# Small decay and rate products in pairs behind the first eight gate tiles of a two-block network

## The chip, the cores and the metric

The kernel runs on one core of one Trainium2 chip. The metric is the device time of one launch in microseconds; lower is better. The core has a matrix engine (TensorE, PE in the profile, its weight loads PEld), a vector engine (VectorE, DVE), an activation engine (ScalarE, ACT), GpSimd (POOL) and SyncE (SP), which issues most DMAs. Each engine works through its own instruction stream in order; engines wait for one another through semaphores.

## The reference

Two blocks run one after the other on a sequence of 1024 tokens of 1024 features, in float32. The second block is where the change lies. Cut to what matters, it starts like this:

```python
h = rmsnorm_2(x, g_mix)
z = h @ w_in                      # 1024 x 5384
zf = z[..., :1544]                # attention ("fox"): q, k, v and 8 forget columns
zr = z[..., 1544:3336]            # recurrence ("rwkv"), 1792 columns
zg = z[..., 3336:]                # two gates of 1024 columns
y_fox = fox_attention(q, k, v, log_sigmoid(zf[..., 1536:] + b_f))
zr = zr + mu_shift * (token_shift(zr) - zr)
dw, da = zr[..., 1536:1600], zr[..., 1600:1664]
w_log = -softplus(-(w0 + tanh(dw) @ w_decay_up)) - 0.5   # decay, 64 -> 512
a = sigmoid(a0 + da @ w_aaa_up)                          # rate, 64 -> 512
y_rwkv = rwkv7_scan(...) ...
merged = sigmoid(zg[..., :1024]) * (y_fox @ w_o_fox) + sigmoid(zg[..., 1024:]) * (y_rwkv @ w_o_rwkv)
x = x + merged @ w_out            # then a feed-forward part and an embedding part
```

The two products with inner size 64 (`dw`, `da`) are the small decay and rate products of the title. All else of the block stays as it is.

## The kernel before, in words

Large products are made in three passes of 512 columns (high weights by high data, low weights by high data, high weights by low data), so a tile of 128 features by 512 tokens with 8 slices of the inner dimension takes 24 matmuls (lines 469 to 471, helper `pe_fm`). Weights come in pieces of 1 MB: SP loads one (`sp_load`, line 407), ACT copies its high part (`ac_cut`, line 420), DVE subtracts to get the low part (`ve_cut`, line 430), and PE may use it. A piece feeds four tiles.

Stage `a4` makes all of `z` in this order: attention columns (`first`), recurrence columns (`shift`, 28 tiles), the small products (`lora`: 16 tiles, four feature groups by two token halves by decay and rate), and the gates (`gates`, 32 tiles, numbered 0 to 31 here). For each small tile PE makes one product with 64 rows (line 2922), ACT takes it out of its PSUM bank with a Sigmoid (line 3033), DVE scales the decay ones (line 2976), and ACT issues a DMA to DRAM (line 3040). Results of `a4` are kept in eight staging slots, taken in turn by the number `no[key]`.

PSUM has 8 banks. A product takes the next bank of a ring (`Banks.take`): `RING` is banks 0 to 5, the gate tiles have a ring of their own (0, 1, 2, 3), the attention has `FB` = (4, 5, 6). Each ring has one place counter for the whole program, kept under the ring's tuple, so two users of the same tuple share a counter. Before it writes, PE waits until the bank's former result was taken out (`bk.room`).

While the gate tiles run, the attention is begun beside them. It is written as one generator for each engine (`pe_fox`, `ve_fox`, `ac_fox`, `po_fox`, `sp_fox`), whose steps count the same on all engines. Each gate tile takes three steps: on PE behind the slices 2, 5 and 7 of the tile, on DVE and ACT ahead of the tile's evacuation (line 2983) and its DMA (line 3048). The first steps are: 1 load and bias the forget columns (ACT line 3332, DVE 3292); 2 their log-sigmoid on ACT (3335 to 3339: Abs, Exp, Ln); 3 the cumulative sum on DVE (3296, 3298). Then, for each of four pairs of heads: rests; the norms of q and k (steps 6 to 13 of the first pair: ACT Square 3348, PE 3272, ACT Ln 3355 and Exp 3360, DVE 3311); then for each of eight query blocks the scores (PE 3152, DVE 3196 and 3201), the minimum (DVE 3208), the Exp (ACT 3228), the transposes (PE 3164) and the weighted sum (PE 3176). In all PE has 228 steps for four pairs, and a tail.

What is left of the attention at the end of `a4` runs in `b2` beside the recurrence. There each step of the other streams is followed by one slot of the attention, slowed so that step n of what is left comes in slot 2.5 n (rounded down):

```python
def slow(stream):
    for n, _ in enumerate(stream):
        yield
        yield
        if n % 2:
            yield
```

The loop of `b2` has 352 slots; the last 13 stand behind the steps of the recurrence's last scan (`ve_scan`, `ac_scan`, `pe_scan` of unit 7). Behind the attention comes its tail (`pe_tail`, `ve_tail`, `ac_tail`, `sp_tail`): rests, and then the first four output tiles of the next stage (`o_tiles[:4]`, PE lines 719 to 721, banks 4 to 7) from four parts, each with a high part (ACT 3445) and a low part (DVE 3435). What does not fit into the loop's slots runs behind it. Then all engines meet, and stage `a5` makes the other output tiles: its first four (`tiles[4:8]`) wait for room in the next four banks of `RING` and then for low parts (DVE 4102); DVE takes the four kept tiles out of banks 4 to 7 (line 4111) behind those low parts.

Of the kernel before, what the change touches and what calls it, by code (L numbers as in the profile page):

```python
# [10 lines left out]
ALU = mybir.AluOpType  # L11
ACT = mybir.ActivationFunctionType
# [231 lines left out]
def program(nc, D, out, S):  # L244
# [3 lines left out]
    with ExitStack() as ctx:  # L248
# [70 lines left out]
        def PC(name, k=0, p0=0, p1=128):  # L319
            return PB[p0:p1, pat[name] + k:pat[name] + k + 1]  # L320
# [16 lines left out]
        bk = Banks(PS, [sem(f"bank_filled{b}") for b in range(8)], [sem(f"bank_emptied{b}") for b in range(8)])  # L337
        RING, SUM0, SUM1 = (0, 1, 2, 3, 4, 5), (6,), (7,)
# [5 lines left out]
        s_o = [dma_sig(f"stage_out{i}") for i in range(8)]  # L344
# [324 lines left out]
        def span(hf):  # L669
            return slice(0, T) if hf is None else slice(512 * hf, 512 * hf + 512)  # L670
# [2184 lines left out]
        def a4(pe_fox, ve_fox, ac_fox, po_fox, sp_fox, load_first):  # L2855
# [6 lines left out]
            WU = AF[:, 10 * T + 6:10 * T + 518]  # L2862
            first = fm("fox_qk", "w_in_2", 0, 1024) + tm("fox_v", "w_in_2", 1024, 512, 8) + fm("fox_f", "w_in_2", 1536, 128)
            shift, gates = fm("shift", "w_in_2", 1544, 1792), fm("gates", "w_in_2", 3336, 2048)
            lora = [(j, hf, g) for j in range(4) for hf in range(2) for g in range(2)]
            no = {t.key: i for i, t in enumerate(first)}
            no.update({("lora",) + u: len(first) + i for i, u in enumerate(lora)})
            no.update({t.key: len(first) + 16 + i for i, t in enumerate(gates)})

            def stage(key):  # L2870
                return AF[:, 512 * (no[key] % 8):512 * (no[key] % 8 + 1)]

            def room(key):
                return s_o[no[key] % 8].at(no[key] // 8 - 1)
# [1 line left out]
            def stored(key):  # L2876
                return s_o[no[key] % 8].at(no[key] // 8)

            def three(stream):
                for _ in range(3):  # L2880
                    next(stream)

            def mix_sums(e):
# [21 lines left out]
            def pe_a4(e):  # L2905
                for n, t in enumerate(first):
                    if t.seg == "fox_v" and t.f + t.a == 0:
                        root_columns(e)
                    (pe_tm if t.seg == "fox_v" else pe_fm)(e, t, hp, parts_ready(2, None) if n == 0 else None)
                    if n == 1:  # L2910
                        mix_sums(e)
                    if n == 4:
                        out_sums(e)
                for t in shift:
                    pe_fm(e, t, hp)
                e.wait_ge(*lora_in.at(1))
                e.wait_ge(*sh_act.at(0))
                for j, hf, g in lora:
                    key = ("lora", j, hf, g)
                    ps, s_ = bk.take(key, RING), slice(64 * g, 64 * g + 64)  # L2920
                    e.wait_ge(*bk.room(key))
                    e.matmul(ps, WU[s_, j * 128:(j + 1) * 128], DD[s_, hf * 512:(hf + 1) * 512], start=True,
                             stop=True).then_inc(*bk.fill(key))
                for t in gates:
                    pe_fm(e, t, hp, None, (0, 1, 2, 3), pe_fox, (2, 5, 7))

            def ve_a4(e):
                ve_cut(e, first[0].j + 2)
# [25 lines left out]
                for t in shift:  # L2954
# [14 lines left out]
                    e.tensor_tensor(d, raw[:, 0:T], raw[:, 1:T + 1], ALU.subtract).then_inc(*vo.up())  # L2969
                    e.wait_ge(*vo.last())  # L2970
                    e.scalar_tensor_tensor(d, d, PC("mu_shift_2", t.f), raw[:, 1:T + 1], ALU.mult, ALU.add).then_inc(*sh_dif.up())
                for u in lora:
                    if u[2] == 0:
                        b = stage(("lora",) + u)
                        e.wait_ge(*bk.emptied(("lora",) + u))
                        e.tensor_scalar(b, b, -math.exp(-0.5), None, ALU.mult).then_inc(*lora_neg.up())
                for t in gates:
                    if t.first:
                        ve_cut(e, t.j + 2)
                    three(ve_fox)  # L2980
                    e.wait_ge(*bk.filled(t.key))
                    e.wait_ge(*room(t.key))
                    e.tensor_tensor(stage(t.key), bk[t.key], RR[:, span(t.hf)], ALU.mult).then_inc(*bk.empty(t.key))

            def ac_a4(e):
                ac_cut(e, first[0].j + 2)
# [10 lines left out]
                for n_, t in enumerate(first):  # L2997
# [5 lines left out]
                    n = t.m if t.seg == "fox_v" else 512  # L3003
# [9 lines left out]
                for t in shift:  # L3013
# [10 lines left out]
                        e.activation(d, d, ACT.Sigmoid).then_inc(*sh_act.up())  # L3024
                        e.wait_ge(*sh_act.at(1))
                    e.dma_start(S["zr"][t.f * 128:(t.f + 1) * 128, :], d).then_inc(*dif_out[0 if t.f == 13 else t.f % 2].up())
                scaled = 0
                for u in lora:
                    j, hf, g = u
                    key = ("lora",) + u  # L3030
                    e.wait_ge(*bk.filled(key))
                    e.wait_ge(*room(key))
                    e.activation(stage(key), bk[key], ACT.Sigmoid, bias=PC(("w0_2", "a0_2")[g], j)).then_inc(*bk.empty(key))
                    if g == 0:
                        e.wait_ge(*lora_neg.at(scaled))
                        scaled += 1
                    else:
                        e.wait_ge(*bk.emptied(key))
                    row = 512 * g + j * 128
                    e.dma_start(S["rw_d"][row:row + 128, hf * 512:(hf + 1) * 512], stage(key)).then_inc(*s_o[no[key] % 8].up())  # L3040
                for t in first[-2:]:
                    e.wait_ge(*stored(t.key))
                for t in gates:
                    if t.first:
                        ac_cut(e, t.j + 2)
                    three(ac_fox)
                    e.wait_ge(*bk.emptied(t.key))
                    e.dma_start(S["gates"][t.f * 128:(t.f + 1) * 128, t.hf * 512:(t.hf + 1) * 512],
                                stage(t.key)).then_inc(*s_o[no[t.key] % 8].up())

            def po_a4(e):
                e.wait_ge(*z_lo.at(piece(2, 7)))
                e.memset(AF[:, 4 * T:4 * T + 3078], 0.0).then_inc(*sh_pad.up())
                for t in gates:
                    three(po_fox)

            def sp_a4(e):
                e.dma_start(WU[0:64, :], D["w_decay_up_2"]).then_inc(*lora_in.up())
                e.dma_start(WU[64:128, :], D["w_aaa_up_2"]).then_inc(*lora_in.up())
                sp_load(e, shift[-1].j + 3)  # L3060
                e.wait_ge(*x_spilled.at(0))
                e.wait_ge(*bk.filled(shift[-1].key))
                for t in first[-8:]:
                    e.wait_ge(*stored(t.key))
                for n, t in enumerate(gates):
                    if t.first:
                        sp_load(e, t.j + 3)
                    three(sp_fox)
# [1361 lines left out]
```

## Time and profile before

| what | us |
|---|---|
| median of 3 runs | 4201.96 (4199.37 to 4202.57) |
| profiled execution, its own time | 4214.02 |
| its span | 4212.7 |
| PE busy | 3892.7 (92%) |
| DVE busy | 2257.0 (54%) |
| ACT busy | 1196.0 (28%) |
| POOL busy | 446.9 (11%) |

The profile shows one execution; its own time is longer than the median of the runs, so it is used for durations and differences, not for the total. In timeline rows the columns are: start in us from the span's start, duration in us, engine and line, operation, what it writes and reads, shapes, count, and in brackets the idle time before it and what ended that. "ACTq" and "SPq" are DMA issues of those engines. Shares of busy time are means over stages with different limits.

### The profile page before, as it was taken

Reading aid. Unit: us, or ns where it says so; the run is one execution under the profiler, and the core shown is the slowest. Engines: PE = TensorE matmul, PEld = TensorE weight load, DVE = VectorE, ACT = ScalarE, POOL = GpSimd, SP = SyncE. Lnnn points to the kernel's source line nnn. Section 1 sums busy time; section 2 is a strip of 40 time slices with the busy share of each in tenths; the row PEclk is TensorE's granted clock in tenths of the full one; section 3 lists DMA queues with packets and bytes.
Section 4 is the critical chain, followed back from the end, with each engine's and each line's share of the span. In section 5 each row is a group of like instructions: output and inputs, shape, how many; then the busy total and the mean of one; then the engine's idle time right before and its main releaser. Section 6 shows DMA issues by size and latency. Waiting matters only on the chain. (4 is left out here: it accounts for less than half of the span.)

```text
span 4212.7 us, 75887 instructions
## 1 busy us (share of the span) xinstructions
PE 3892.7 (92%) x33370; PEld 3190.3 (76%) x33370; DVE 2257.0 (54%) x3662; ACT 1196.0 (28%) x1700; POOL 446.9 (11%) x440
## 2 busy tenths in 40 slices
PE   6999969988999999999999898788888999999999
PEld 5888847777867788888798576566677788888877
DVE  4643335554434666766634233564544476676673
ACT  4221234433323433121400323333323321111132
POOL 0001103321000432000000001222212000000000
PEclk8999979997999999999999899886879999999999
DMA  5211120113121334322322322111004211111111
GB/s 181 82 61 57 57 93 7 33 33 134 40 80 70 104 114 168 130 86 82 118 88 90 131 84 68 56 36 45 23 30 163 89 41 50 50 44 47 50 46 65
DMA packets 228061, 318.71 MB, mean 76 GB/s; under 512 B 17149, under 2 KB 172541, under 8 KB 227605
## 3 DMA queue, kind: packets, MB, share of 16 engines
q1 hardware_dynamic: 199088, 251.13, 18.1%
q10 hardware_dynamic: 28644, 62.72, 3.9%
q8 instruction: 265, 4.34, 0.4%
q14 instruction: 64, 0.52, 0.0%
HBM read 235.46 MB, written 78.35 MB: 74 GB/s over the span
## 5 line engine op out<-in xcount | busy, mean ns | idle before, releaser
L469 PE MATMUL ps<-sb_a_h,sb_whi 128*128 128x512 f32 (+1 forms) x2336 | 932.7, 399 | 6.1 <-DVE sb_wlo L430 5.7
L471 PE MATMUL ps<-sb_a_h,sb_whi 128*128 128x512 f32 (+1 forms) x2336 | 915.5, 392 | 0.0
L470 PE MATMUL ps<-sb_a_h,sb_wlo 128*128 128x512 f32 (+1 forms) x2336 | 915.2, 392 | 0.0
L469 PEld LDWEIGHTS ps<-sb_a_h,sb_whi 128*128 128x128 f32 (+1 forms) x2336 | 441.8, 189 | 116.5 <-issue 16.3
L470 PEld LDWEIGHTS ps<-sb_a_h,sb_wlo 128*128 128x128 f32 (+1 forms) x2336 | 442.0, 189 | 95.2 <-issue 5.1
L471 PEld LDWEIGHTS ps<-sb_a_h,sb_whi 128*128 128x128 f32 (+1 forms) x2336 | 441.1, 189 | 95.2
L420 ACT ACTIVATE sb_whi<-sb_wraw 128x2048 fp32r<-128x2048 f32 (+3 forms) x132 | 233.7, 1771 | 810.2 <-PE ps L471 493.9
L675 DVE TENSOR_TENSOR sb_x<-sb_x,ps 128x512 f32<-128x512 f32 x480 | 314.8, 684 | 211.5 <-PE ps L471 196.5
L430 DVE TENSOR_TENSOR sb_wlo<-sb_wraw,sb_whi 128x2048 fp32r<-128x2048 f32 (+3 forms) x132 | 281.9, 2136 | 223.7 <-ACT sb_whi L420 203.2
L469 PE MATMUL ps<-sb_a_g,sb_whi 128*128 128x512 f32 x896 | 349.8, 390 | 11.5 <-DVE sb_x L675 10.5
L470 PE MATMUL ps<-sb_a_g,sb_wlo 128*128 128x512 f32 x896 | 348.7, 389 | 0.0
L471 PE MATMUL ps<-sb_a_g,sb_whi 128*128 128x512 f32 x896 | 348.6, 389 | 0.0
L469 PEld LDWEIGHTS ps<-sb_a_g,sb_whi 128*128 128x128 f32 x896 | 168.2, 188 | 50.6 <-DVE sb_x L675 14.7
L471 PEld LDWEIGHTS ps<-sb_a_g,sb_whi 128*128 128x128 f32 x896 | 168.2, 188 | 35.0
L470 PEld LDWEIGHTS ps<-sb_a_g,sb_wlo 128*128 128x128 f32 x896 | 168.2, 188 | 34.8
L4226 DVE TENSOR_TENSOR sb_a_f<-ps,sb_root 128x512 f32<-128x512 f32 x88 | 60.9, 692 | 101.8 <-PE ps L471 96.1
L3245 POOL TENSOR_TENSOR sb_b<-sb_x,sb_consts 128x128 f32<-128x128 f32 x64 | 30.0, 483 | 611.2 <-DMA sb_x<-fox_c 398.9
L4276 ACT ACTIVATE sb_a_g<-sb_a_f 128x512 fp32r<-128x512 f32 x44 | 27.8, 633 | 226.0 <-DVE sb_a_f L4246 226.0
L526 PE MATMUL ps<-sb_a_h,sb_whi_blocks 128*128 128x512 f32 x224 | 87.9, 392 | 4.0 <-DVE sb_wlo_blocks L552 4.0
L528 PE MATMUL ps<-sb_a_h,sb_whi_blocks 128*128 128x512 f32 x224 | 87.9, 392 | 0.0
L527 PE MATMUL ps<-sb_a_h,sb_wlo_blocks 128*128 128x512 f32 x224 | 87.7, 391 | 0.0
L719 PE MATMUL ps<-sb_a_h,sb_whi 128*128 128x512 f32 x128 | 56.4, 441 | 25.2 <-DVE sb_wlo L430 8.7
(589 smaller groups left out, 6692.0 us busy)
## 6 DMA issues: line engine op xcount, KB each, us to landing
sb_wraw<-w_in SPq DMA_DIRECT2D x33, 1024.0 KB, 5.3
sb_wraw<-w_ff SPq DMA_DIRECT2D x32, 1024.0 KB, 5.4
sb_wraw<-w_up SPq DMA_DIRECT2D x22, 1024.0 KB, 5.1
sb_wraw<-w_down SPq DMA_DIRECT2D x11, 1024.0 KB, 4.9
sb_wraw<-w_xkv SPq DMA_DIRECT2D x8, 1024.0 KB, 5.5
sb_wraw<-w_out SPq DMA_DIRECT2D x8, 1024.0 KB, 5.3
sb_b<-rw_d SPq DMA_DIRECT2D x16, 512.0 KB, 6.4
sb_b<-y SPq DMA_DIRECT2D x16, 512.0 KB, 5.8
```

The source lines that it names most:

```text
L420: e.activation(WH[j % 2][:, 0:m], WR[j % 2][:, 0:m], ACT.Copy).then_inc(s_whi, 1)
L430: e.tensor_tensor(WL[j % 2][:, 0:m], WR[j % 2][:, 0:m], WH[j % 2][:, 0:m].bitcast(F32), ALU.subtract).then_inc(s_wlo, 1)
L469: e.matmul(o, wh[:, k, c], xh[:, sl], start=(k == 0), stop=False)
L470: e.matmul(o, wl[:, k, c], xh[:, sl], start=False, stop=False)
L471: m = e.matmul(o, wh[:, k, c], xl[:, sl], start=False, stop=(k == t.nk - 1))
L526: e.matmul(o, wh[:, k, :], xhi, start=(opens and k == 0), stop=False, skip_group_check=True)
L527: e.matmul(o, wl[:, k, :], xhi, start=False, stop=False, skip_group_check=True)
L528: m = e.matmul(o, wh[:, k, :], xlo, start=False, stop=(k == 3), skip_group_check=True)
L675: e.tensor_tensor(o, o, bk[t.key], ALU.add).then_inc(*bk.empty(t.key))
L719: e.matmul(ps[n], wh[:, k, c], xh[:, sl], start=(i == 0), stop=False)
L3245: e.tensor_tensor(nms[g], R(NCB[g] + qb * 128, 128), C("causal"), ALU.subtract).then_inc(*fx_nm[g].up())
L4226: e.tensor_tensor(raw[:, 2:514], bk[t.key], RR[:, span(t.hf)], ALU.mult).then_inc(*bk.empty(t.key))
```

## The change

The 16 small tiles no longer stand between `shift` and `gates`. Gate tile 0 follows the shift tiles at once; behind each of the gate tiles 0 to 7 stands one pair (decay and rate of one feature group and token half), on every engine behind that tile's own work. The pairs use the ring (4, 5, 6), the attention's, in place of `RING`. On ACT both Sigmoids of a pair come first, then its two DMAs. Beside gate tile 0 only one step of the attention is taken (on PE behind slice 7); the other tiles take three as before, so the steps 2, 3, ... come two steps later in the order of gate tiles. The first load of the recurrence's inputs on SP moves from gate tile 8 to gate tile 12. The staging slots are numbered anew.

In `ve_a4` the scaling of a pair's decay tile moves behind the evacuation of gate tile n in the same way as the pair on ACT below, and `po_a4` and `sp_a4` take `fox_steps` in place of `three`. The diff's core, from the tables, `pe_a4`, `ac_a4` and `sp_a4`:

```diff
-            lora = [(j, hf, g) for j in range(4) for hf in range(2) for g in range(2)]
+            lora, LORA = [(j, hf, g) for j in range(4) for hf in range(2) for g in range(2)], (4, 5, 6)
             no = {t.key: i for i, t in enumerate(first)}
-            no.update({("lora",) + u: len(first) + i for i, u in enumerate(lora)})
-            no.update({t.key: len(first) + 16 + i for i, t in enumerate(gates)})
+            beside = {n: lora[2 * n:2 * n + 2] for n in range(8)}
+            for n, t in enumerate(gates):
+                no[t.key] = len(no)
+                no.update({("lora",) + u: len(no) + i for i, u in enumerate(beside.get(n, ()))})
...
-            def three(stream):
-                for _ in range(3):
+            def fox_steps(stream, n):
+                for _ in range(3 if n else 1):
                     next(stream)
...
-                e.wait_ge(*lora_in.at(1))
-                e.wait_ge(*sh_act.at(0))
-                for j, hf, g in lora:
-                    key = ("lora", j, hf, g)
-                    ps, s_ = bk.take(key, RING), slice(64 * g, 64 * g + 64)
-                    e.wait_ge(*bk.room(key))
-                    e.matmul(ps, WU[s_, j * 128:(j + 1) * 128], DD[s_, hf * 512:(hf + 1) * 512], start=True,
-                             stop=True).then_inc(*bk.fill(key))
-                for t in gates:
-                    pe_fm(e, t, hp, None, (0, 1, 2, 3), pe_fox, (2, 5, 7))
+                for n, t in enumerate(gates):
+                    pe_fm(e, t, hp, None, (0, 1, 2, 3), pe_fox, (2, 5, 7) if n else (7,))
+                    if n == 0:
+                        e.wait_ge(*lora_in.at(1))
+                        e.wait_ge(*sh_act.at(0))
+                    for j, hf, g in beside.get(n, ()):
+                        key = ("lora", j, hf, g)
+                        ps, s_ = bk.take(key, LORA), slice(64 * g, 64 * g + 64)
+                        e.wait_ge(*bk.room(key))
+                        e.matmul(ps, WU[s_, j * 128:(j + 1) * 128], DD[s_, hf * 512:(hf + 1) * 512], start=True,
+                                 stop=True).then_inc(*bk.fill(key))
...
-                scaled = 0
-                for u in lora:
-                    j, hf, g = u
-                    key = ("lora",) + u
-                    e.wait_ge(*bk.filled(key))
-                    e.wait_ge(*room(key))
-                    e.activation(stage(key), bk[key], ACT.Sigmoid, bias=PC(("w0_2", "a0_2")[g], j)).then_inc(*bk.empty(key))
...
-                for t in gates:
+                for n, t in enumerate(gates):
                     if t.first:
                         ac_cut(e, t.j + 2)
-                    three(ac_fox)
+                    fox_steps(ac_fox, n)
                     e.wait_ge(*bk.emptied(t.key))
                     e.dma_start(S["gates"][t.f * 128:(t.f + 1) * 128, t.hf * 512:(t.hf + 1) * 512],
                                 stage(t.key)).then_inc(*s_o[no[t.key] % 8].up())
+                    for j, hf, g in beside.get(n, ()):
+                        key = ("lora", j, hf, g)
+                        e.wait_ge(*bk.filled(key))
+                        e.wait_ge(*room(key))
+                        e.activation(stage(key), bk[key], ACT.Sigmoid, bias=PC(("w0_2", "a0_2")[g], j)).then_inc(*bk.empty(key))
+                    for j, hf, g in beside.get(n, ()):
+                        key = ("lora", j, hf, g)
+                        e.wait_ge(*(bk.emptied(key) if g else lora_neg.at(n)))
+                        row = 512 * g + j * 128
+                        e.dma_start(S["rw_d"][row:row + 128, hf * 512:(hf + 1) * 512], stage(key)).then_inc(*s_o[no[key] % 8].up())
...
-                    if n == 8:
+                    if n == 12:
                         for d in dif_out:
                             e.wait_ge(*d.last())
```

## Rows read from the trace of the kernel before

**Rows 1.** The first line of the page: span and instructions.

```profile
span 4212.7 us, 75887 instructions
```

**Rows 2.** Busy time of each engine in two stretches of stage a4 (us, count).

```profile
2329.00:2349.50 20.50, 17.58 (x34) 6.10 (x33) 5.76 (x9) 8.65 (x13) 0.00 (x0) 0.63 0.79 282
2349.50:2396.00 46.50, 35.45 (x124) 26.20 (x123) 14.69 (x14) 23.88 (x23) 0.87 (x2) 0.83 0.32 105
```

**Rows 3.** Timeline of PE from the small products to the third query block.

```profile
2329.07 2.85 PE L2922 MATMUL ps<-sb_a_f 64*128 64x512 f32 x12
...
2349.46 0.79 PE L469 MATMUL ps<-sb_a_h,sb_whi 128*128 128x512 f32 x1
...
2354.72 0.40 PE L469 MATMUL ps<-sb_a_h,sb_whi 128*128 128x512 f32 x1
...
2364.73 0.39 PE L471 MATMUL ps<-sb_a_h,sb_whi 128*128 128x512 f32 x1
2372.73 1.22 PE L3272 MATMUL ps<-sb_x,sb_consts 128*128 128x512 f32 x1 [7.61 <-ACT sb_x L3348]
...
2395.94 0.89 PE L3152 MATMUL ps<-sb_x 64*128 64x128 f32 x4 [2.26 <-DVE sb_x L3311]
...
2416.90 0.92 PE L3152 MATMUL ps<-sb_x 64*128 64x384 f32 x4
```

**Rows 4.** Groups of ACT instructions by line: the Sigmoids of the small products.

```profile
L3033 ACT ACTIVATE sb_a_f<-ps,sb_params 128x512 f32<-128x512 f32 x16 | 11.0, 687 | 11.0 <-DVE sb_a_f L2976 7.4 <-ACT sb_a_f L3033 3.2 <-ACT sb_a_f L3024 0.5
```

**Rows 5.** Timeline of ACT, first steps of the attention, and one Exp.

```profile
2333.67 0.33 ACTq L3026 DMA_DIRECT2D zr<-sb_a_f  x1
...
2356.19 1.92 ACT L420 ACTIVATE sb_whi<-sb_wraw 128x2048 fp32r<-128x2048 f32 x1 [0.54 <-ACT sb_a_f L3033]
...
2362.26 1.28 ACT L3337 ACT_TABLE_LOAD   x1
...
2365.93 1.15 ACT L3339 ACTIVATE sb_b<-sb_b,sb_consts 8x1024 f32<-8x1024 f32 x1
...
2371.62 1.06 ACT L3348 ACTIVATE sb_x<-sb_x 128x1024 f32<-128x1024 f32 x1 [4.54 <-DVE sb_a_f L2983]
...
2419.29 0.62 ACT L3228 ACTIVATE sb_x<-sb_x,sb_b 128x384 f32<-128x384 f32 x1 [6.47 <-DVE sb_b L3208]
```

**Rows 6.** Timeline of DVE, cut, forget columns, first evacuations of gate tiles.

```profile
2358.14 2.29 DVE L430 TENSOR_TENSOR sb_wlo<-sb_wraw,sb_whi 128x2048 fp32r<-128x2048 f32 x1 [3.63 <-ACT sb_whi L420]
...
2360.42 0.73 DVE L3292 TENSOR_SCALAR sb_b<-sb_b,sb_params 8x1024 f32<-8x1024 f32 x1
...
2368.36 2.28 DVE L3298 TENSOR_TENSOR_SCAN sb_b<-sb_consts,sb_b 8x1024 f32<-8x1024 f32 x1
2370.56 1.25 DVE L2983 TENSOR_TENSOR sb_a_f<-ps,sb_root 128x512 f32<-128x512 f32 x2
```

**Rows 7.** Timeline of PE, scores of the last attention step but one in a4.

```profile
2608.61 1.13 PE L3152 MATMUL ps<-sb_x 64*128 64x512 f32 x4
```

**Rows 8.** Timeline of ACT at the end of the loop of b2.

```profile
3161.55 1.99 ACT L3445 ACTIVATE sb_a_h<-sb_b 128x1024 fp32r<-128x1024 f32 x2
...
3166.46 0.21 ACT L4003 ACTIVATE sb_b<-sb_b 128x8 f32<-128x8 f32 x1
```

**Rows 9.** Timeline of DVE at the end of the loop of b2.

```profile
3171.00 0.69 DVE L3990 TENSOR_TENSOR sb_b<-sb_b,ps 128x512 f32<-128x512 f32 x1 [1.40 <-POOL sb_b L4022]
```

**Rows 10.** Timeline of PE, the first output tiles, ahead of the meeting.

```profile
3163.99 0.77 PE L719 MATMUL ps<-sb_a_h,sb_whi 128*128 128x512 f32 x1 [5.46 <-DVE sb_a_h L3435]
...
3177.54 0.39 PE L721 MATMUL ps<-sb_a_h,sb_whi 128*128 128x512 f32 x1
```

**Rows 11.** Timeline of DVE at the start of a5.

```profile
3186.47 2.36 DVE L4102 TENSOR_TENSOR sb_a_h<-sb_b,sb_a_h 128x1024 fp32r<-128x1024 f32 x2
3188.98 2.48 DVE L4111 TENSOR_TENSOR sb_x<-sb_a_f,ps 128x512 f32<-128x512 f32 x4
```

**Rows 12.** Timeline of PE at the start of a5.

```profile
3186.61 0.79 PE L719 MATMUL ps<-sb_a_h,sb_whi 128*128 128x512 f32 x1 [8.69 <-DVE sb_wlo L430]
```

More of the change, by code:

```diff
@@ L2971, in ve_a4 @@
                     e.scalar_tensor_tensor(d, d, PC("mu_shift_2", t.f), raw[:, 1:T + 1], ALU.mult, ALU.add).then_inc(*sh_dif.up())
-                for u in lora:
[L2973 to L2976, printed above, removed]
-                for t in gates:
+                for n, t in enumerate(gates):
                     if t.first:
                         ve_cut(e, t.j + 2)
-                    three(ve_fox)
+                    fox_steps(ve_fox, n)
                     e.wait_ge(*bk.filled(t.key))
@@ L2983, in ve_a4 @@
                     e.tensor_tensor(stage(t.key), bk[t.key], RR[:, span(t.hf)], ALU.mult).then_inc(*bk.empty(t.key))
+                    for u in beside.get(n, ()):
+                        if u[2] == 0:
+                            b = stage(("lora",) + u)
+                            e.wait_ge(*bk.emptied(("lora",) + u))
+                            e.tensor_scalar(b, b, -math.exp(-0.5), None, ALU.mult).then_inc(*lora_neg.up())
             def ac_a4(e):
@@ L3026, in ac_a4 @@
                     e.dma_start(S["zr"][t.f * 128:(t.f + 1) * 128, :], d).then_inc(*dif_out[0 if t.f == 13 else t.f % 2].up())
-                scaled = 0
-                for u in lora:
-                    j, hf, g = u
-                    key = ("lora",) + u
-                    e.wait_ge(*bk.filled(key))
-                    e.wait_ge(*room(key))
-                    e.activation(stage(key), bk[key], ACT.Sigmoid, bias=PC(("w0_2", "a0_2")[g], j)).then_inc(*bk.empty(key))
[L3034 to L3040, printed above, removed]
                 for t in first[-2:]:
                     e.wait_ge(*stored(t.key))
-                for t in gates:
+                for n, t in enumerate(gates):
                     if t.first:
                         ac_cut(e, t.j + 2)
-                    three(ac_fox)
+                    fox_steps(ac_fox, n)
                     e.wait_ge(*bk.emptied(t.key))
@@ L3053, in po_a4 @@
                 e.memset(AF[:, 4 * T:4 * T + 3078], 0.0).then_inc(*sh_pad.up())
-                for t in gates:
-                    three(po_fox)
+                for n, t in enumerate(gates):
+                    fox_steps(po_fox, n)
             def sp_a4(e):
@@ L3067, in sp_a4 @@
                         sp_load(e, t.j + 3)
-                    three(sp_fox)
-                    if n == 8:
+                    fox_steps(sp_fox, n)
+                    if n == 12:
                         for d in dif_out:
```

## The prediction

> **What bounds the kernel now.** First the page: one execution spans 4212.7 us [rows 1], its own time is 4214.02, 12.1 us (0.29%) above the median of the runs. So I forecast a difference from the trace and add it to 4201.96. Then the windows of stage a4: over the small products PE is busy 17.58 of 20.5 us, at a mean granted clock of 0.63; in the next 46.5 us 35.45, at 0.83 [rows 2]. The clock has two levels, 1.2 and 2.4 GHz, so these stretches are mixtures. Then PE's timeline [rows 3]. The reader sees three losses: the small products take from 2329.07 to 2349.46, 20.4 us; the first gate products then come at the lower level (12 in 5.26 us, 0.438 each; later 44 in 10.01, 0.2275 each); and PE stands 7.61 us ahead of the attention's first norm product at 2372.73, and 2.26 ahead of the second head's scores at 2395.94. What I call a lower-clock spell below is those 12 products: 12 x 0.21 = 2.5 us, with the pair 2.6.
>
> Why the small products are slow stands in the ACT groups: 16 Sigmoids of 687 ns, 11.0 us busy, and 11.0 idle, mostly behind DVE's scaling [rows 4]. PE's own part is about 4 x 0.24 a pair, 0.95 us (estimate from the 0.2275 product), 7.6 us in all.
>
> **Term A, the lead at the first scores.** After the change PE starts gate tile 0 at 2329.07. ACT is free at 2334.0 (the last recurrence DMA, 2333.67 + 0.33), cuts for 1.92 [rows 5], DVE subtracts 2.29 and adds the bias 0.73 [rows 6]: 2339.0. Evacuating tile 0 (half of 1.25) and issuing its DMA (0.33) gives 2340.0, two Sigmoids 1.4, two DMA issues 0.7: 2342.2. The log-sigmoid with its two table loads takes 5.9 (from 2361.15, where the bias ends, to 2367.08, where Ln ends [rows 5, 6]): 2348.1. Two DVE operations up to the end of the cumulative sum take 3.56 (2367.08 to 2370.64): 2351.6. Tile 1's evacuation and DMA, 1.1; a Sigmoid table load, by the load seen, 1.28; two Sigmoids and two issues 2.1; the Square 1.06: PE's norm product comes at about 2357.2, in place of 2372.73. PE arrives there with 66 products and two pairs, 16.9 us, at about 2347 with some lower clock: it stands some 10 us.
>
> From there ACT has eight table loads (10.3), a cut (1.9), six Sigmoids (4.1), nine issues (3.0), norm Lns and Exps (4.6 at 1.15) and a Square (1.1), with DVE's evacuations (1.9) between: 27 us, to the second head's scores at 2384.4. These need a bank of (4, 5, 6) that the pair of tile 4 must leave first, behind tile 4's evacuation. Before it was 2395.94: 11.5 us earlier. The work left there differs too: 639 gate products in place of 654 (-3.4), three pairs more (+2.9), two attention steps fewer in a4 (-1.8, worked out under D): -2.3. Term A: **-13.8** (-8 if the pair's waits take one more evacuation round each of 2.75 us, -16 without the spells).
>
> A rule of the Trainium skill speaks against this change: "ScalarE: Activation LUTs", section "What ACT_TABLE_LOAD costs", has a switch of tables as a load of about 1.28 us and a drain of 1.38. The trace shows the load, 1.28, but not the drain: from 2362.26 to 2367.08, 4.82 us hold two loads (2.56), an Exp and a Ln (1.15 each) [rows 5], with nothing left for two drains. By the page the seven loads added on PE's path would be 9.7 us dearer.
>
> **Term B, gate tile 8.** A new weight piece begins there. After the change the third query block's scores stand at the end of tile 7 and its Exp in tile 8, so the cut stands between them. Before, scores at 2416.90 and Exp at 2419.29 are 2.4 apart [rows 3, 5]. After, ACT and DVE put between them: evacuation 0.7, DMA 0.4, two Sigmoids 1.4, issues 0.8, the cut 1.92, DVE's low part 2.29: 7.5 us. PE's cover is pair 7 and 18 products, 0.95 + 4.1. The transposes behind the Exp (0.62) with DVE's minimum ahead wait about 4.4, and a lower-clock spell of 2.6 follows: **+7.0**. Nothing if the rest finds cover (DVE may have evacuated early), +9 if the spell is twice as long.
>
> **Term C, gate tile 24.** The same for the second pair's block, without a Sigmoid pair: 7.5 - 2.2 less PE's 4.1 and what the engines are ahead, about 1.9, with or without a spell of 2.6. Before, PE loses there in other places, which I can't sort: **+2** (-1 to +4).
>
> **Term D, two attention steps more beside the recurrence.** The steps of a4 are 2 fewer, and b2's loop has 134 in place of 132. The last scores in a4 take 1.13 [rows 7], with the softmax's other product some 0.7: 1.8 us of PE leave a4 (credited in A) and return in b2. If they run there at full clock beside other waits they cost nothing or 1.8, at the lower clock 3.7: **+2** (0 to 3.7).
>
> **Term E, the tail's order.** Two steps later is five slots later. Before, ACT's high parts of the kept output tiles (3161.55, 1.99) come ahead of the Exp at 3166.46 of the last scan's gate [rows 8], and PE's first output product at 3163.99 [rows 10]; DVE's last gate multiply ends at 3171.69, held by POOL [rows 9]. The loop has 13 slots after the last scan. The copies go from slot 345 to 350, behind ACT's Ln and Exp; PE's output products from 347 to 352, behind the loop, behind the gate's transposes. DVE's low parts come behind its last gate multiply. With the last scan's chain a little earlier (ACT no longer has 1.99 us of copies in front of it): multiply done at 3169.3, low part of the first slice at 3170.6, PE starts then in place of 3163.99: 6.6 later, less some 1.2 us of transposes that no longer stand in between (they are done in the wait). The last output product at 3177.54 goes to about 3183: **+5.7** (0, if low parts come as early as now, to +7).
>
> **Term F, banks at the start of a5.** The small products no longer take from RING. 16 takes of six banks shift the place counter by 4, so where the first tiles of a5 took banks 0 to 3, they take 2, 3, 4, 5. Banks 4 and 5 hold kept output tiles until DVE's evacuation at 3188.98 (four in 2.48 us, 0.62 each), behind the low parts [rows 11]. PE, which began at 3186.61, released by DVE's cut [rows 12], now begins when two of them are out: the four tiles go slice by slice together, so the last of the four banks rules: 3188.98 + 1.27 = 3190.25. **+3.7** (0, if PE is late there for another reason, to +4.5 with a slower first spell).
>
> **Costed at nothing.** POOL's steps (its first work is step 14). The SP load of the recurrence's inputs, four tiles later: some 20 tiles of 5.46 us are left before its first use, 109 us; without that cover it would cost its tile delay of 22 us. SP's queue: the pieces' loads stand ahead of that step in both orders. The pairs' DMAs, 16 before and after; if the DMAs, busy 0.79 in the first stretch [rows 2], delay the forget columns, that is up to 2 us of A. Staging slots: 8, each reused at least 2.7 tiles (15 us) later. DVE's scaling, 0.43 by half an evacuation and less, stands behind an evacuation with PE several products ahead; if uncovered it is 0.4 a pair, 3.2 in eight.
>
> **The sum.** -13.8 + 7.0 + 2.0 + 2.0 + 5.7 + 3.7 = +6.6 us: 4201.96 + 6.6 = **4208.6**, 0.16% slower, inside the 0.2% (8.4 us) that a measurement here can tell from no change. Chance of this case 0.55.
>
> **Rivals.**
> *The recurrence loop pays by the step* (slower, 0.17): from 2608.61 to 3163.99 are 555 us for 132 steps, 4.2 each [rows 7, 10]. If the loop is as long as its steps, two cost 8.3 in place of 2: +12.9, 4214.9. For it: the products behind the loop wait for the steps. Against: the loop's end is the scan's (POOL releases the last multiply [rows 9]). From D above 3.8 the result is beyond 0.2%.
>
> *Each table switch costs about its load again* (slower, 0.04): seven loads more on PE's path, 7 x 1.28 = 9.0: +15.6, 4217.6. Against it the 4.82 us above. The page named there would make it +16.3.
>
> *Tiles 8 and 24 have cover* (0.16): B and C fall away, -2.4: 4199.6. For it: PE has three tiles in the gate ring of four banks to run ahead. Against: steps bind PE's order to ACT's.
>
> *The ends are not on the path* (0.08): E and F fall away, +6.6 - 9.4 = -2.8: 4199.2. For it: PE waits 8.69 at a5's start for a weight cut [rows 12], so a late tail could be hidden. Against: all engines meet between the two. With both last rivals: -11.8, 4190.2, faster.
>
> **Range and chances.** 4198 to 4218: below it lie the cases where lead stays and two or more charges fail, above it those where the loop's step price and the upper bounds meet. The likeliest case's own range is 4201 to 4214. Slower by over 0.2% (4210.4): 0.22 of the likeliest case, 0.15 of the loop rival, 0.04: 0.41. Faster (4193.6): 0.08 out of the last two. The rest 0.51.
>
> **What would show it.** A: PE's norm product (line 3272) near 2357, waiting some 10 us for the Square; second head's scores near 2384; about 11 ACT table loads more in the page's group. B: the transposes in tile 8 waiting some 4 us for the Exp, and a lower clock behind. C: the same, smaller, in tile 24. D: the loop of b2 longer by 0 to 4 us between its meetings. E: the first output product (line 719) behind the last gate multiply, the meeting some 5.7 us later after the scan's end. F: the first product of a5 released by DVE's evacuation (line 4111), not by a cut (line 430). The prediction is wrong if the norm product stays past 2365 (then A is half), or if the loop shows a price by the step.

## The result, and the profile after

The changed kernel ran at a median of 4222.87 us (4211.84 to 4238.99, 8 runs), the kernel before beside it at 4201.94 (4192.71 to 4215.83): ratio 1.0049, interval 1.0033 to 1.0066, 14 to 28 us slower. A second set of runs (below) gave 1.0033 (1.0011 to 1.0054). The forecast of 4208.6 and its range up to 4218.0 were too low.

The profiled executions are 15.5 us apart [rows 1]:

```profile
span 4228.2 us, 75898 instructions
```

Where do they part? Five marks cut the span in both traces: G, the last weight cut ahead of the gates; S, the recurrence's first scan in b2; R, the last product of its last unit; C, the first weight cut of a5 on ACT; P, a5's first product [rows 12]. In the kernel before (start, duration, engine and line) G, S, R and C are

```profile
2311.25 1.92 ACT L420 ACTIVATE sb_whi<-sb_wraw 128x2048 fp32r<-128x2048 f32 x1 [19.85 <-DVE sb_a_f L2971]
2619.92 1.22 DVE L3613 TENSOR_TENSOR_SCAN sb_b<-sb_consts,sb_b 128x512 f32<-128x512 f32 x1
3152.40 1.60 PE L3902 MATMUL ps<-sb_b 64*64 64x64 f32 x26
3184.07 1.04 ACT L420 ACTIVATE sb_whi<-sb_wraw 128x1024 fp32r<-128x1024 f32 x1
```

and in the changed kernel

```profile
2315.85 1.92 ACT L420 ACTIVATE sb_whi<-sb_wraw 128x2048 fp32r<-128x2048 f32 x1 [19.84 <-DVE sb_a_f L2974]
2620.41 1.22 DVE L3612 TENSOR_TENSOR_SCAN sb_b<-sb_consts,sb_b 128x512 f32<-128x512 f32 x1
3156.14 1.60 PE L3901 MATMUL ps<-sb_b 64*64 64x64 f32 x26
3193.57 1.04 ACT L420 ACTIVATE sb_whi<-sb_wraw 128x1024 fp32r<-128x1024 f32 x1
```

The stretch up to G is 4.6 us longer, and the change does not touch it: executions of one program differ there (copies of the kernel before reach G at 2306.7 and 2312.8). G to S is 4.1 shorter, S to R 3.2 longer, R to C 5.7 longer, C to P 4.0 longer. What follows P is 2.0 longer, but 2.0 longer in a copy of the kernel before as well.

**Stage a4.** PE's timeline, the answer to [rows 3]:

```profile
2364.22 2.07 PE L3271 MATMUL ps<-sb_x,sb_consts 128*128 128x512 f32 x2 [7.88 <-ACT sb_x L3347]
...
2392.53 0.79 PE L3151 MATMUL ps<-sb_x 64*128 64x128 f32 x2
...
2425.26 1.54 PE L3163 MATMUL ps<-sb_consts,sb_x 128*128 128x128 f32 x6 [3.32 <-ACT sb_x L3227]
```

and windows (PE, PEld, DVE, ACT, POOL busy, the granted clock third from the end), the answer to [rows 2]:

```profile
2329.00:2349.00 20.00, 19.05 (x78) 13.43 (x77) 7.36 (x9) 4.24 (x4) 0.00 (x0) 1.00 0.54 173
2349.00:2369.00 20.00, 12.12 (x33) 7.21 (x33) 5.10 (x5) 13.36 (x14) 0.87 (x2) 0.67 0.46 152
2409.00:2429.00 20.00, 16.66 (x70) 12.00 (x69) 6.06 (x16) 8.02 (x13) 0.91 (x2) 0.88 0.18 66
2429.00:2449.00 20.00, 20.00 (x96) 16.33 (x96) 5.22 (x16) 2.52 (x6) 0.93 (x2) 0.86 0.07 27
```

The first 20 us run at full clock where the small products had 0.63, and the norm product comes 13.1 us earlier after G. Then PE stands for the Square, and at gate tile 8 for the Exp. What stands ahead of that Exp is seen on ACT and DVE, merged by time:

```profile
2418.06 1.27 ACT L3043 ACTIVATE sb_a_f<-ps,sb_params 128x512 f32<-128x512 f32 x2 [6.52 <-DVE sb_a_f L2981]
...
2420.15 1.92 ACT L420 ACTIVATE sb_whi<-sb_wraw 128x2048 fp32r<-128x2048 f32 x1 [0.83 <-ACT sb_a_f L3043]
2422.09 1.28 ACT L3227 ACT_TABLE_LOAD   x1
2424.49 0.61 ACT L3227 ACTIVATE sb_x<-sb_x,sb_b 128x384 f32<-128x384 f32 x1 [1.12 <-DVE sb_b L3207]
```

```profile
2422.10 2.29 DVE L430 TENSOR_TENSOR sb_wlo<-sb_wraw,sb_whi 128x2048 fp32r<-128x2048 f32 x1 [2.89 <-ACT sb_whi L420]
2424.31 0.21 DVE L3207 TENSOR_REDUCE sb_b<-sb_b 128x1 f32<-128x2 f32 x2
```

Sigmoids, cut, DVE's low part, the minimum, the Exp. In the kernel before no cut stood ahead of that minimum: ACT had been idle for 6.47 us when the Exp came [rows 5].

**The tail and a5.** ACT, DVE and PE, the answers to [rows 8] to [rows 12]:

```profile
3168.30 0.21 ACT L4002 ACTIVATE sb_b<-sb_b 128x8 f32<-128x8 f32 x1
3168.42 3.88 ACT L3444 ACTIVATE sb_a_h<-sb_b 128x1024 fp32r<-128x1024 f32 x4
```

```profile
3172.53 0.69 DVE L3989 TENSOR_TENSOR sb_b<-sb_b,ps 128x512 f32<-128x512 f32 x1 [1.39 <-POOL sb_b L4021]
3173.13 4.62 DVE L3434 TENSOR_TENSOR sb_a_h<-sb_b,sb_a_h 128x1024 fp32r<-128x1024 f32 x4
...
3198.57 2.56 DVE L4110 TENSOR_TENSOR sb_x<-sb_a_f,ps 128x512 f32<-128x512 f32 x4 [0.24 <-ACT sb_a_f L4136]
```

```profile
3174.49 0.76 PE L719 MATMUL ps<-sb_a_h,sb_whi 128*128 128x512 f32 x1 [2.38 <-DVE sb_a_h L3434]
...
3187.19 0.39 PE L721 MATMUL ps<-sb_a_h,sb_whi 128*128 128x512 f32 x1
...
3200.10 0.77 PE L719 MATMUL ps<-sb_a_h,sb_whi 128*128 128x512 f32 x1 [12.53 <-DVE sb_x L4110]
```

The high parts come behind the Exp, not ahead of it; the low parts behind the last gate multiply; the first output product 1.3 us behind that multiply's end, where it was 7.7 ahead. And a5's first product is released by the evacuation of the kept tiles, not by a cut.

### The profile page after: what moved, and what is told of

Same layout as the page of the kernel before. It is cut to its first block and busy times, and to the rows that moved or that the text cites. A ratio compares the mean times of both kernels' runs of the same rounds, so it can differ in the third digit from the quotient of the medians.

```text
span 4228.2 us, 75898 instructions
## 1 busy us (share of the span) xinstructions
PE 3899.4 (92%) x33370; PEld 3196.7 (76%) x33370; DVE 2257.5 (53%) x3662; ACT 1210.4 (29%) x1711; POOL 447.5 (11%) x440
## 5 line engine op out<-in xcount | busy, mean ns | idle before, releaser
L469 PE MATMUL ps<-sb_a_g,sb_whi 128*128 128x512 f32 x896 | 349.8, 390 | 11.5 <-DVE sb_x L675 10.5
L3244 POOL TENSOR_TENSOR sb_b<-sb_x,sb_consts 128x128 f32<-128x128 f32 x64 | 31.9, 512 | 643.9 <-DMA sb_x<-fox_c 382.7
```

The costliest lines, as they stand in the source:

```text
L469: e.matmul(o, wh[:, k, c], xh[:, sl], start=(k == 0), stop=False)
L3244: e.tensor_tensor(nms[g], R(NCB[g] + qb * 128, 128), C("causal"), ALU.subtract).then_inc(*fx_nm[g].up())
```

## The experiments

The kernels ran in five sets on three chips, 12 runs of each kernel; each ratio is against the 23 to 35 runs of the kernel before in the same set (`after` is the result above, 8 runs against 8). The stretches between the marks are of each kernel's one trace, in us.

The column "equal clock" takes out what goes with the granted clock. For every run the mean granted clock of TensorE is on record. In each set the times fall along one straight line with it, for all kernels alike, by 2.9 to 3.1 us for each 0.001 of the clock, and scatter by 2.2 to 3.0 us about it. The column gives how far a kernel's line lies above that of the kernel before in its set, in us; two standard errors are 1.6 to 2.2 us. For `after` the runs of the kernel before beside it have no clock on record, so it is held against all 163 others. What a kernel gains or loses by the clock itself is not in this column.

| kernel | ratio (interval) | equal clock | G-S | S-R | R-C | C-P |
|---|---|---|---|---|---|---|
| before | 1 | 0 | 308.7 | 532.5 | 31.7 | 2.5 |
| control_before | 1.0011 (0.9994, 1.0029) | +0.6 | 308.8 | 523.3 | 32.7 | 2.5 |
| control_again | 1.0015 (0.9995, 1.0035) | +1.3 | 305.7 | 518.1 | 31.7 | 2.5 |
| after | 1.0049 (1.0033, 1.0066) | +13.4 | 304.6 | 535.7 | 37.4 | 6.5 |
| again_after | 1.0033 (1.0011, 1.0054) | +12.4 | 304.4 | 529.2 | 37.5 | 6.4 |
| shift_alone | 1.0016 (0.9999, 1.0033) | +5.2 | 304.5 | 529.3 | 37.3 | 2.5 |
| pairs_three_steps | 1.0014 (0.9994, 1.0034) | +4.5 | 307.1 | 527.4 | 31.7 | 6.4 |
| after_banks_tail | 1.0016 (0.9999, 1.0033) | +4.4 | 301.8 | 525.2 | 31.9 | 2.5 |
| after_banks_tail_again | 1.0021 (1.0005, 1.0036) | +4.5 | 304.4 | 535.8 | 32.0 | 2.5 |
| shift_tail | 1.0021 (1.0005, 1.0037) | +1.9 | 301.3 | 538.9 | 32.1 | 2.5 |
| pairs_three_steps_banks | 0.9997 (0.9983, 1.001) | +1.5 | 307.1 | 520.6 | 31.5 | 2.5 |
| loop_five_more | 0.9998 (0.9985, 1.0011) | -5.2 | 298.3 | 524.3 | 32.2 | 2.5 |
| after_banks_aligned | 1.0014 (1.0, 1.0028) | +0.6 | 308.2 | 527.0 | 33.1 | 2.5 |
| shift_aligned | 1.0005 (0.9988, 1.0021) | -2.7 | 308.5 | 520.2 | 32.9 | 2.5 |
| before_delayed | 1.0022 (1.0004, 1.004) | +2.9 | 304.9 | 525.7 | 32.0 | 2.5 |
| before_delayed_again | 1.001 (0.9992, 1.0029) | +3.4 | 301.7 | 535.0 | 32.3 | 2.5 |
| pairs_banks_delayed | 1.0019 (1.0003, 1.0034) | +6.9 | 302.9 | 522.9 | 32.3 | 2.5 |
| before_delayed_ten | 0.9968 (0.995, 0.9986) | -8.3 | 303.4 | 523.0 | 29.5 | 2.5 |
| before_delayed_ten_again | 0.9965 (0.9947, 0.9983) | -7.6 | 304.9 | 528.1 | 29.6 | 2.5 |
| pairs_banks_delayed_ten | 0.9968 (0.9953, 0.9983) | -3.9 | 303.3 | 526.2 | 29.6 | 2.5 |

Four things are to be seen first. R to C and C to P can be read from one trace: R to C is 31.5 to 33.1 with the tail in its old slots (29.5 in the three kernels with ten slots) and 37.3 to 37.5 with it five slots later, C to P 2.5, or 6.4 to 6.5 with the banks shifted. G to S is less sure: three traces of the kernel before give 308.7, 308.8 and 305.7. S to R can't be read so: the same three give 532.5, 523.3 and 518.1. And an unchanged copy came out at 1.0011 and 1.0015, so a ratio below about 1.002 says nothing by itself; at equal clock the copies are at +0.6 and +1.3, and about 2 us can be told apart.

**Copies.** No edit.

> The kernel before, unchanged: a second profile of it and the spread of its own ratio. Every theory: ratio 1.000, within 0.1% (4202, plus or minus 5 us). The stages of its trace should stand within 2 us of those of the first one outside the two recurrences; how far they differ in the recurrences is what is looked for.

> The kernel before, unchanged, once more, as the measure of what a ratio of equal kernels shows on this chip: 1.000, within 0.15%. If it stands near 1.002, the ratios of the delayed kernels say nothing.

> The changed kernel once more. Theory of the terms (lead of about 12 us at gate tile 4, lost by gate tile 9; then 3 for the loop, 5.8 for the tail, 4 for the banks, 1.6 later): its own trace adds up to +10.9 us outside the first block, so 4213. Rival (what the two traces show is not all, another cost comes in most executions): 4218 to 4225 again, and a second trace in which one stage is some 10 us longer than in the first.

The second copy's G to S misses the 2 us that were expected of it. In its trace the kernel is 3.0 us ahead of the other two from gate tile 5 on: ten microseconds that ran at a granted clock of 0.72 and 0.73 in those ran at 1.00 in this one, behind the same wait. A difference of this size in a4 between two traces need not be a kernel's.

The second trace of the changed kernel gave the same a4, tail and a5 within 0.2 us. The ratio fell between the two theories. At equal clock the two sets agree, +13.4 and +12.4, nearer to the +10.9 of the first theory than to the rival's.

**The parts of the change.** The shift alone: the small products stay ahead of the gates, and one attention step stands beside gate tile 0 (on the other engines likewise).

```diff
-                for t in gates:
-                    pe_fm(e, t, hp, None, (0, 1, 2, 3), pe_fox, (2, 5, 7))
+                for n, t in enumerate(gates):
+                    pe_fm(e, t, hp, None, (0, 1, 2, 3), pe_fox, (2, 5, 7) if n else (7,))
```

The pairs alone: the changed kernel with

```diff
-                for _ in range(3 if n else 1):
+                for _ in range(3):
-                    pe_fm(e, t, hp, None, (0, 1, 2, 3), pe_fox, (2, 5, 7) if n else (7,))
+                    pe_fm(e, t, hp, None, (0, 1, 2, 3), pe_fox, (2, 5, 7))
```

> The small products ahead of the gates as in the kernel before, only the attention's first steps a tile later (one step beside gate tile 0). No lead, no pairs, banks of the first output tiles as before. Theory of the terms: 3 (loop) + 5.8 (tail) + 1 to 3 (the cut now between scores and Exp in tile 8, without Sigmoids): +10 to +12 us, 4213. Rival A (the loop is dear by the step or by its new alignment): +18 us or more, 4220. Rival B (the shift costs nothing, all comes from the pairs): +0, 4202.

> The changed kernel, but with three attention steps beside gate tile 0 as before, so the attention keeps its place in the order of gate tiles and its tail its slots; only the pairs and the banks are changed. Theory of the terms: the lead of some 10 us is kept past tile 8, since scores and Exp of the third query block stand in one tile; banks +4: -6 us, 4196. Rival (the pairs themselves eat the lead, by table loads on ACT and the waits they bring): -2 + 4 = +2 us, 4204, or more.

The lead was read from DVE's evacuations of the gate tiles (end of each, counted from G, less the kernel before; the last row is a copy of the kernel before):

| gate tile | 0 | 4 | 7 | 8 | 9 | 16 | 20 | 23 | 30 | 31 |
|---|---|---|---|---|---|---|---|---|---|---|
| after | -29.1 | -13.6 | -10.3 | -5.6 | -1.6 | -7.2 | -0.1 | 0.0 | 0.3 | -3.5 |
| shift_alone | -9.4 | -5.8 | -8.2 | -5.6 | -1.6 | -7.2 | -0.1 | 0.0 | 0.3 | -3.5 |
| pairs_three_steps | -19.9 | -7.0 | -3.5 | -1.1 | -1.6 | -1.6 | -1.6 | -1.6 | -1.6 | -1.6 |
| control_again | 0.0 | -1.6 | -3.0 | -3.0 | -3.0 | -3.0 | -3.0 | -3.0 | -3.0 | -3.0 |

The shift alone has the same course from tile 8 on as the whole change, to 0.1 us: in a4 the pairs bring nothing beside it. Where an attention step stands in a tile moves its evacuation too (the -7.2 at tile 16; PE's first product of that tile is 1.8 us ahead). Up to tile 30 nothing of the lead is left, and PE's first product of tile 31 is 0.5 us behind. Only the last evacuation is 3.5 ahead, where two attention steps fewer have gone before: what a4 gains is not the lead, it is the work of these two steps.

The pairs alone lose their lead without any cut between scores and Exp: the time that PE no longer spends among the small products comes back as waits on the Sigmoids and what is behind them. On PE in that kernel:

```profile
2362.43 2.07 PE L2927 MATMUL ps<-sb_a_f 64*128 64x512 f32 x2 [11.44 <-ACT sb_a_f L3043]
...
2381.74 2.08 PE L3271 MATMUL ps<-sb_x,sb_consts 128*128 128x512 f32 x2 [3.27 <-ACT sb_x L3347]
```

The theory of the terms expected 10 us kept here; 1.6 were, less than two copies of the kernel before differ by, and the rival was right for the lead. The tail is as before in this kernel, and a5 late by 3.9; with the shift alone it is the other way round, the tail late by 5.6. The shift alone was put at +10 to +12 us and came out 6.7 above the kernel before by the medians, 5.2 at equal clock; at equal clock both its rivals, +18 and 0, are off.

**Tail and banks undone.** The changed kernel with

```diff
                 for t in shift:
                     pe_fm(e, t, hp)
+                bk.spot[RING] += 16
...
-            TAIL = 5
+            TAIL = 3
```

and, beside it, the shift alone with `TAIL` 3 (`shift_tail`) and the pairs alone with the counter set on (`pairs_three_steps_banks`).

> The changed kernel with two undone parts: RING's place counter set on by 16 where the small products took from it, and two rests fewer ahead of the tail, so that its steps come in their old slots. Theory of the terms: the trace's tail stage goes back by 5.6 us (first output product 7.7 us ahead of the last gate multiply's end, as before, not 1.3 behind it) and the start of a5 by 4.0; a4 keeps its 4.2; left is -4.2 plus what the loop costs (D, 0 to 4): -4 to 0, 4203 to 4207 beside a before of 4207. Rival (the loop pays by the step, 8 us): +4, 4211 or more, with the tail and a5 stages back as well.

> The changed kernel with banks and tail undone once more, on the chip of the aligned kernels. Theory Z: ratio 1.0015 again, 8 to 11 us above the aligned one. If it comes out at 0.999, what was laid to the loop is the spread between sets of runs, and no cost.

> The attention's shift alone (small products ahead of the gates) with two rests fewer ahead of the tail. By the trace of the shift alone a4 is 4.1 us shorter and the tail is back to the length before: -4.1 + D, the same time as the kernel with pairs, banks and tail undone, within 2 us. If the pairs are worth something that the trace of a4 doesn't show, this one is slower by it. Loop against before: 0 to +4 by the theory of the terms, +8 by the rival that it pays by the step.

> Pairs beside the gates, three attention steps beside gate tile 0, RING's counter set on by 16: no step moves into the loop, tail and a5 as before. Theory of the terms: -1.6 in a4, first product of a5 back by 3.9, nothing else: -1.6, 4205 beside a before of 4207; its loop as long as the loops of before (523 to 533). Rival: no lead at all is left, 4207 to 4209.

On PE in the first of these the two products stand where they did before: 

```profile
3154.56 0.77 PE L719 MATMUL ps<-sb_a_h,sb_whi 128*128 128x512 f32 x1 [5.46 <-DVE sb_a_h L3435]
...
3177.41 0.79 PE L719 MATMUL ps<-sb_a_h,sb_whi 128*128 128x512 f32 x1 [8.54 <-DVE sb_wlo L430]
```

R to C and C to P are back, 5.5 and 4.0 us. The times agree: the mean ratio of the two sets of the changed kernel, 1.0041, less that of these two, 1.00185, is 0.00225, 9.5 us; at equal clock it is 8 to 9. What is left, 4.4 and 4.5 us at equal clock where -4 to 0 was expected, is in neither the tail nor a5. The pairs with three steps and restored banks are as fast as the kernel before.

**The loop of b2.** Five steps fewer at the end of a4, `TAIL` 0 (the `three` of tile 30 takes one step, that of tile 31 none):

> The kernel before with five attention steps fewer at the end of a4 (none beside the last gate tile, one beside the last but one) and five rests fewer ahead of the tail, so that five steps more run in b2's loop and the tail stays in its slots; nothing else is changed. Theory of the terms: PE's work of five steps (3 to 5 us) leaves a4 and comes back in the loop in part: 0 to +4, 4207 to 4211 beside a before of 4207. Rival (the loop pays 4.2 us by the step): 21 in the loop less 4 in a4: +17, 4224.

No price of 4.2 us by the step, which was put at +17 us: G to S is shorter by 10.4 (7.4 against control_again), the ratio 0.9998. One thing is not held fixed here: five steps more also put the attention's later steps twelve slots later, and by the ten slots below that alone may be worth some 8 us. Even so the step costs less than the rival says: -5.2 at equal clock, with 7.4 to 10.4 back from G to S and 8 back for the slots, leaves 10 to 13 us for five steps, 2.0 to 2.6 each (an estimate from these numbers). Next, alignment: the attention in the loop waits five slots first, with `TAIL` 3, in the kernel before and in the pairs with restored banks; or, the other way round, the two added steps are taken at once and `TAIL` stays 5, in the changed kernel with the counter set on and in the shift alone.

```diff
             def slow(stream):
+                for _ in range(5):
+                    yield
                 for n, _ in enumerate(stream):
```

```diff
             def slow(stream):
+                for _ in range(2):
+                    next(stream)
                 for n, _ in enumerate(stream):
```

> The kernel before, with nothing changed in a4; in b2 the attention waits five slots ahead of its first step and its tail has two rests fewer, so that every attention step stands at the same slot of the recurrence as in the changed kernel and the tail stays where it is. Theory Z (what the loop costs beyond the sums seen in a4, tail and a5 comes from the new alignment of the two streams): +8 to +11 us, ratio about 1.002. Theory W (it comes from the work of the two added steps, or is no cost of the loop at all): 0, ratio 1.000.

> The kernel before with the attention five slots later in b2's loop and nothing else, once more. Theory Z (the alignment costs): ratio 1.001 to 1.003 again. Theory W (no cost, the first 1.0022 was spread between sets of runs): 1.000, within 0.1%.

> Pairs beside the gates, three steps beside gate tile 0, banks restored (0.9997 before), with the attention five slots later in the loop. Theory Z: 4 to 9 us more than without the delay, ratio 1.001 to 1.002. Theory W: 0.9997.

> The changed kernel with RING's counter set on by 16, and in b2 the attention's first two steps taken at once, so that all later steps and the tail stand at the same slots as before. Theory Z: -4 to -6 us in a4, the loop as before, ratio 0.999, and 8 to 11 us faster than the kernel with banks and tail undone. Theory W: like that one, ratio 1.0015.

> The shift alone (small products ahead of the gates) with the two steps taken at once at the loop's start, as in the other kernel. Theory Z: -4 to -6 us, ratio 0.999, the same as the aligned kernel with pairs within 2 us, since the pairs bring nothing in a4 beside the shift. Theory W: ratio 1.002.

Five slots came out at 1.0022, 1.0010 and 1.0019, the copies at 1.0011 and 1.0015: by the ratios alone a price of five slots is not shown. At equal clock it is. Five slots in the kernel before are +2.9 and +3.4 beside the copies' +0.6 and +1.3; in the pairs with restored banks +6.9 beside +1.5; and the aligned kernels, with the slots put back, lie 3.9 below the changed kernel with banks and tail undone (+0.6, +4.4 and +4.5) and 4.6 below the shift with its tail undone (-2.7, +1.9). So five slots cost some 3 to 5 us. Why, these runs don't show.

The aligned kernels came out at 1.0014 and 1.0005, and not at the 0.999 that was expected. With the two steps taken ahead of it, the recurrence's first scan comes 3.9 us later: from DVE's last evacuation of a gate tile to the scan are 9.7 us, in both of them, against 5.8 in the changed kernel and in the shift alone. In the aligned shift DVE copies the transposes of the second step, which PE made behind ACT's Exp, just ahead of the scan:

```profile
2616.28 0.69 DVE L3215 COPY sb_x<-ps 128x512 f32<-128x512 f32 x1 [3.07 <-PE ps L3164]
2616.88 1.21 DVE L3613 TENSOR_TENSOR_SCAN sb_b<-sb_consts,sb_b 128x512 f32<-128x512 f32 x1
```

So the 4.1 us that a4 seemed to gain are two attention steps that were put off. A shorter G to S is no gain by itself: in all kernels with five or ten slots of delay the scan comes 4.0 us earlier than in their base (2.4 us behind the last evacuation, in place of 6.4), though nothing was changed in a4, since the attention's first step no longer stands ahead of it; and those with five slots are slower.

Ten slots (`range(10)`, `TAIL` 1):

> The kernel before with the attention ten slots later in b2's loop (tail with four rests fewer, so in its old slots). Theory Z allows any value, since the streams meet differently; if the cost grows with the delay, 1.003 to 1.005. Theory W: 1.000.

> The kernel before with the attention ten slots later in b2's loop, once more. Theory Z (where the attention's steps meet the recurrence's sets the loop's length): ratio 0.995 to 0.998 again. Theory W (the alignment is worth nothing, 0.9968 was a lucky set): 1.000 to 1.0015, as the two unchanged copies.

> Pairs beside the gates, three steps beside gate tile 0, banks restored, with the attention ten slots later. Theory Z: the gain of the ten slots on top of the 1.6 us of a4: 0.996 to 0.997, faster than both kernels. Theory W: 0.9997.

0.9968, 0.9965 and 0.9968 on two bases: where the two streams meet does have a price, and here ten slots are worth some 13 to 15 us. These kernels beat both others. At equal clock 8.3, 7.6 and, against the pairs with restored banks, 5.4 us of it are left; the rest goes with a higher granted clock. 2.1 us of it is seen in R to C, at a granted clock of 0.83 in place of 0.71; windows of the kernel before and of the first delayed one from R to C:

```profile
3152.00:3184.00 32.00, 19.66 (x147) 16.63 (x145) 13.22 (x17) 9.45 (x11) 1.45 (x2) 0.71 0.17 63
```

```profile
3145.00:3174.00 29.00, 16.77 (x128) 13.82 (x123) 13.08 (x17) 9.46 (x11) 1.33 (x2) 0.83 0.36 137
```

Where the other 11 to 13 us come from, one trace of each can't tell: their S to R, 523.0 to 528.1, lies among those of the kernel before. The executions that were traced are also among the longest of their sets (4204.16, 4205.87 and 4200.95, with medians of 4188.44, 4191.86 and 4196.48).

## Why the prediction was wrong

**Term A, right in course, wrong in what stayed.** The norm product came 13.1 us earlier (15.5 forecast) after a wait of 7.88 (10), and the second head's scores 8.0 earlier, 11.2 in the second trace (11.5). ACT made 21 table loads between G and the end of the gates in place of 10, the 11 more that were forecast. No drain was seen behind a load or ahead of one (the load in tile 8 starts 0.02 us behind the cut's end), so the rival by the Trainium skill's "ScalarE: Activation LUTs", section "What ACT_TABLE_LOAD costs", does not hold in this trace: a load of 1.28 us and the Sigmoid that follows it at once are

```profile
2359.69 1.28 ACT L3043 ACT_TABLE_LOAD   x1 [4.59 <-DVE sb_a_f L2981]
2360.98 1.27 ACT L3043 ACTIVATE sb_a_f<-ps,sb_params 128x512 f32<-128x512 f32 x2
```

**Terms B and C, right in place.** The Exp of tile 8 made PE wait 3.32 us, with a clock of 0.88 and 0.86 around it; the lead fell by 8.7 from tile 7 to 9 (7.0). The forecast was 4.4, though the pieces that it names, 7.5 and the Exp's 0.62 less PE's 5.05, add up to 3.1. The same wait is in the shift alone (3.22 us), so the Sigmoids were not its cause. The pairs alone, with scores and Exp in one tile, have no wait of PE there: the cut between scores and Exp was. In tile 24 PE waited 1.80 us for the Exp (1.9 forecast),

```profile
2559.99 0.33 PE L3163 MATMUL ps<-sb_consts,sb_x 128*128 128x128 f32 x1 [1.80 <-ACT sb_x L3227]
```

and tiles 24 to 27 took it 3.1 us longer than before (2).

A, B and C together gave -4.1 (-4.8), and that they agree is luck. The forecast has 3.0 us of lead left and 1.8 of PE's work for the two steps; of the lead nothing was left by tile 30, and the two steps were worth all of it. It went in pieces: 3.3 us between tiles 4 and 7, which no term has, 1.7 more than forecast at tile 8 and 1.1 more in tiles 24 to 27.

**Term D, the step that failed.** "If they run there at full clock beside other waits they cost nothing or 1.8, at the lower clock 3.7": +2 was forecast for the loop. With tail and banks undone the kernel is at +4.4 and +4.5 at equal clock, with 4.1 gained in a4, so the loop costs 8.5. Two things make it up. The two steps were priced as PE work; they are a chain through DVE, ACT and PE, and at the loop's start they put off the recurrence by 3.9 us. By the same mistake A had credited their leaving with 1.8, so this part evens out. The part that does not was put at nothing without a reason: all 132 steps that follow move five slots against the recurrence, and that costs 3 to 5 us here, where ten slots gain. That the sum is near the 8.3 us of the rival that pays by the step is no proof of it: in the kernel before five slots cost +2.9 and +3.4 with no step added.

**Terms E and F, right.** 5.7 us (5.7 forecast) and 4.0 (3.7), by the mechanisms named, and both undone at will. Rivals three (cover in tiles 8 and 24) and four (the ends off the path) fell with them.

So at equal clock the change costs some 13 us: 9.7 from E and F, where 9.4 was forecast, and about 4 from the rest, where -2.8 was: 3 us of lead that did not stay, and five slots that were not counted. That alone would make about 4215, inside the range. The remainder of the 20.9 us in the first set, 7 or 8, goes with the granted clock: its eight runs have a mean of 0.9425, the runs of the kernel before 0.9445, which at 3 us for each 0.001 is 6 us. The range had no room for such a spread between sets; whether the change lowers the clock by itself is not shown (in the second set it was 0.0004 lower).

## What to carry to other kernels

Work that fills an idle place on one engine has to be followed to the end of the stage: here a lead of 14 us at gate tile 4 was down to 2 at tile 9 and gone before the last tile, as PE came to wait for the same ACT and DVE. Work that leaves a stage is no gain until the stage that takes it in has been read too. When a step moves out of one stage, look at all that counts steps or turns: the tail's slots, and a shared counter of banks, cost 9.7 us with no word of them in the change. When two streams are interleaved by a fixed pace, try a few offsets: ten slots gained 13 to 15 us, and five cost 3 to 5. When one kernel's runs spread by more than the effect, compare them at the same granted clock before calling the effect noise, and say what the comparison leaves out.

## What was not expected of the hardware

The time of one program goes with the granted clock of the whole execution: of the 12 runs of control_again the fastest took 4192.91 us at a mean clock of 0.949, the slowest 4229.61 at 0.937. The correlation of time and clock within the 12 runs of a kernel is -0.81 to -0.99. The stretch that differs most between executions is the second recurrence, where PE works in 64 x 64 pieces: S to R spread over 14 us in three traces of the kernel before, 532.5 us at a granted clock of 0.78, 523.3 at 0.80 and 518.1 at 0.82, while the stretch from P to the end differed by 2.0. And the same wait does not always end the same way: behind one in a4, two executions of the kernel before ran ten microseconds at 0.72 and 0.73, and a third at 1.00, which is worth 3.0 us.
